# Samples' attention with the queries as weights in four column groups, a cache copy by batches, and a seventh chunk split ahead in the output projection

## The chip, the cores and the metric

The kernel runs on one core of one Trainium2 chip, in fp32 throughout. The metric is the device time of one execution in microseconds (us); three runs of the kernel before gave a median of 2682.03 us. TensorE (PE) multiplies, VectorE (DVE) and ScalarE (ACT) do elementwise work and empty the accumulators in PSUM, GpSimd (POOL) adds and issues DMAs, SyncE (SP) issues the loads of the weights.

## What is computed

Two decoder layers over 288 tokens: a prompt of 256 and 32 new sample tokens (8 batches of 4). Per layer:

```
n = RMSNorm(x)
q_s, k_s, v_s, q_r, k_r, v_r, g_r = split(n @ w_in)
o_swa = attention of q_s over k_s, v_s, window 128, 8 heads on 2 key/value heads, bias and sinks
o_ret = gated retention of q_r, k_r, v_r with a state per head (4 heads)
h = x + [o_swa || o_ret] @ w_o
x = h + SwiGLU(RMSNorm(h) @ w_gate_up) @ w_down
```

A sample token attends to 128 cached keys of its own batch (cache_k_win, cache_v_win) and to the new keys of its batch, with softmax over both and a sink. Outputs are y, the new windows of keys and values (for the samples: the cache shifted by 4 rows, then the 4 new rows) and the retention states.

## The kernel before

**The weight stream.** All products with weights have the weights at rest (128 x 128) and the 288 tokens moving. To keep fp32 accuracy, weights and activations are split in a high and a low part (`w_hi`, `w_lo`, `xg_hi`, `xg_lo`), and each block takes three matmuls (L982, L984, L986). The weights come in *rounds*: one round is 256 output columns over 2048 rows, in 8 *chunks* of 12 matmuls. SP loads, ACT writes `w_hi` (L363), DVE subtracts to get `w_lo` (L650), and PE multiplies. `w_hi` and `w_lo` are rings of four: chunk j can only be split once PE is through chunk j - 4. `split(r, j0, j1)` on ACT and on DVE splits chunks j0 to j1 of round r, and each engine's program is an order written by hand, in which the other work stands between the splits. `GLEAD` = 6 is the number of chunks of the next round that are split before that other work.

**The head groups.** After the first six rounds of w_in, a loop over four groups g runs four rounds (r to r + 3) per group. Between their chunks PE does the small matmuls of two attention heads, of the samples of two batches, and of one retention head. For the samples PE transposes the cached keys (`kcT`, L1096), ACT copies them out; PE multiplies with the keys at rest and 16 query columns moving (`sampT`, L1109), ACT copies that; PE transposes it back and adds the scores against the new keys (`samp_s`, L1117, L1119). DVE adds bias and mask and takes the maximum, ACT the exponential, DVE normalises. PE transposes the probabilities (`samp_pT`, L1134, L1135) and multiplies with the values at rest (`samp_pv`, L1142, L1147), which gives the output with the head's dimension on the partitions, as `cat_hi` and `cat_lo` want it. Small fp32 matmuls appear in the trace as two records each, transposes as one. All small results go through PSUM banks 4 to 7, whose users are listed in `BANK_USES`.

**The output projection.** Eight rounds r0 + R_O + 0 to 7 multiply `cat` by w_o. After each round DVE adds the accumulator to the residual (L909, semaphore `x_new`), ACT makes `xg_hi` (L375) and the squares (`pair_tmp`, L383), DVE makes `xg_lo` (L662), POOL adds the squares to `sq_acc` (L1306, L1308, semaphore `sq_added`, for which ACT's next squares wait). Then come the two gate/up rounds of FFN chunk 0 and a sum over partitions (L999).

**POOL's queue.** Per group it loads the bias, the cached keys and values and the states, and stores the new states. After the last group it copies the two cache windows from DRAM to DRAM in two DMAs of 992 KB (L1421), clears `sq_acc` (L1432) and enters the loop of additions.

Of the kernel before, what the change touches and what calls it, by code (L numbers as in the profile page):

```python
# [32 lines left out]
P = 128  # L33
# [3 lines left out]
DB = 8  # L37
# [33 lines left out]
for _name, _n in (("ident", P), ("ones", P), ("eps", 1), ("gammaC", RH), ("kdecay", RH * 2),  # L71
                  ("head_rows", 64), ("cos", T), ("sin", T), ("decay", RH * NP), ("qdecay", RH * NS), ("decay_s", RH * NS),
# [9 lines left out]
    "group": (("s0", 4), ("kcT", 5), ("s1", 4), ("sampT", 6), ("pT0", 5), ("samp_s", 6), ("pT1", 5),  # L82
              ("pv0", 6), ("pv1", 7), ("samp_pT", 5), ("samp_pv", 4), ("state_q", 6), ("o0", 6), ("o1", 7), ("kr_tok", 5),
# [26 lines left out]
def hybrid_trunk(nc, xT, cache_k, cache_v, state, rel_bias, w_in, sinks, sinksT, w_o, gainsT, w_gate_up,  # L110
# [4 lines left out]
    with ExitStack() as ctx:  # L115
        def sb(name, shape, dt=F32):
            return ctx.enter_context(nc.sbuf_tensor(name, shape, dt))
# [14 lines left out]
        sink_s = sb("sink_s", [64, DEPTH])  # L132
        bias_s = sb("bias_s", [64, P + NS])
# [29 lines left out]
        kc = over("kc", [P, 2, PAIR])  # L163
        vc = over("vc", [P, 2, PAIR])
        samp_sT = over("samp_sT", [P, 64])

        state_o = nc.alloc_sbuf_tensor_at("state_o", [P, PAIR], F32, offset=at[0])
        samp_p = over("samp_p", [64, P + NS])
        samp_pT = over("samp_pT", [P, 64])
        samp_pnT = over("samp_pnT", [NS, 64])  # L170
# [20 lines left out]
        kcT = over("kcT", [P, 4, P])  # L191
# [16 lines left out]
        def table(name, parts=P):  # L208
            a, b = TABLES[name]
            return cst[0:parts, a:b]  # L210

# [144 lines left out]
        def _(act):  # L356
# [60 lines left out]
            nc.scalar.activation(sink_s[:], ps[0:64, 5, 0:DEPTH], ACT.Copy).then_inc(bank_read[5], 1)  # L417
            act.drain().then_inc(rows_ready, 1)

            with act.Fori(0, DEPTH) as layer:  # L420
# [25 lines left out]
                with act.Fori(0, RH) as g:  # L446
# [14 lines left out]
                    filled(act, "kcT", layer, g)  # L461
                    copy_out(kcT[:], "kcT", 512)
# [12 lines left out]
                    def normalise(h):  # L475
# [11 lines left out]
                    filled(act, "sampT", layer, g)  # L487
                    copy_out(samp_sT[:], "sampT", 64)
# [6 lines left out]
                    nc.scalar.activation(samp_p[:], samp_p[:], ACT.Exp, bias=stats[0:64, 21:22],  # L495
                                         accum_out=stats[0:64, 22:23])
                    nc.scalar.activation(stats[0:64, 23:24], stats[0:64, 21:22], ACT.Exp,
# [17 lines left out]
                    copy_out(samp_pT[:], "samp_pT", 64, done=False)  # L515
                    copy_out(samp_pnT[:], "samp_pT", 64, NS, 64)
                    split(r + 2, 7, 8)
                    split(r + 3, 0, 1)
                    filled(act, "samp_pv", layer, g)
                    steady(act)  # L520
# [1002 lines left out]
```

## Time and profile before

| | |
|---|---|
| runs | 2682.03 us median (2680.91 to 2684.40, n = 3) |
| the profiled execution | 2685.05 us, its span 2683.5 us, mean granted clock 0.995 |
| PE busy | 2630.4 us, 98% |
| DVE, ACT, POOL busy | 56%, 47%, 7% |
| one group of the loop | 71.0 us, eight in all |
| output projection, first matmul to the sum for the FFN's norm | 127.6 us (layer 0), 124.7 us (layer 1) |

The page lists busy time by engine, the chain of work that ended last, and the groups of instructions with the idle time ahead of them. A matmul's own duration overlaps the next one's, so what a matmul costs in a stream is the distance from start to start: it is read from rows in order of time.

### The profile page before, as it was taken

The numbers are of one execution on the slowest core, as the hardware profiler recorded it, in microseconds if no ns is written. First come the engines' busy times: TensorE is split into PE (matmuls) and PEld (weight loads), VectorE is DVE, ScalarE is ACT, GpSimd is POOL, SyncE is SP. The second block draws the span as 40 slices with busy tenths as digits, with TensorE's granted clock in tenths as the row PEclk, the third lists the DMA queues.
The fourth block names the chain that finished last, engine by engine and source line by source line (L and its number), as shares of the span: only waits on it lengthen the run. The fifth ranks groups of instructions, "written<-read, shape, count | busy, mean of one in ns | idle before, by whom it ended". The sixth has DMA issues, their size and how long they took to land.

```text
span 2683.5 us, 53800 instructions
## 1 busy us (share of the span) xinstructions
PE 2630.4 (98%) x19722; PEld 2596.1 (97%) x19722; DVE 1491.9 (56%) x2387; ACT 1249.6 (47%) x2237; POOL 174.5 (7%) x222
## 2 busy tenths in 40 slices
PE   6999999999999999999999999999999999999997
PEld 6999999999999999999999999999999999999997
DVE  6566665555555555444455666555555555545445
ACT  4455554444444444444444555444444444444443
POOL 5300001000000000000020000110000000000000
PEclk9999999999999999999999999999999999999998
DMA  6655555555555555555555555554555555555554
GB/s 209 202 196 188 186 175 174 160 165 164 162 169 164 157 171 164 160 164 162 163 184 168 192 195 194 186 161 153 171 164 164 164 164 164 164 159 163 164 168 141
DMA packets 429939, 459.02 MB, mean 171 GB/s; under 512 B 19349, under 2 KB 418029, under 8 KB 429872
## 3 DMA queue, kind: packets, MB, share of 16 engines
q1 hardware_dynamic: 407488, 404.38, 49.2%
q0 software_dynamic: 18400, 48.42, 5.3%
q10 hardware_dynamic: 3984, 5.34, 0.6%
q8 instruction: 41, 0.67, 0.1%
q14 instruction: 26, 0.21, 0.0%
HBM read 436.12 MB, written 27.54 MB: 173 GB/s over the span
## 4 chain that ended last, share of the span: by engine, by line
PE 60%; issue 33%; DVE 3%; DVEq 1%; DMA 1%; POOLq 1%; ACT 1%; ACTq 0%; POOL 0%; SPq 0%
PE ps L982 19%; PE ps L984 18%; PE ps L986 18%; DVE w_lo L650 1%; DVE xg_lo L662 1%; DMA new_rs<-st 1%; PE ps L1223 1%; PE ps L1160 1%; PE ps L1232 1%; DVEq L910 1%; DMA raw<-w_in 0%; PE ps L1181 0%; ACT w_hi L363 0%; PE ps L1147 0%; POOLq L1309 0%
## 5 line engine op out<-in xcount | busy, mean ns | idle before, releaser
L650 DVE TENSOR_TENSOR w_lo<-raw,w_hi 128x512 fp32r<-128x512 f32 x1572 | 1067.3, 687 | 910.9 <-ACT w_hi L363 892.6
L363 ACT ACTIVATE w_hi<-raw 128x512 fp32r<-128x512 f32 x1572 | 960.9, 620 | 1105.3 <-PE ps L986 1085.8
L982 PE MATMUL ps<-xg_hi,w_hi 128*128 128x288 f32 x4224 | 1259.2, 298 | 18.7 <-DVE w_lo L650 14.5
L984 PE MATMUL ps<-xg_lo,w_hi 128*128 128x288 f32 x4224 | 1249.2, 296 | 0.0
L986 PE MATMUL ps<-xg_hi,w_lo 128*128 128x288 f32 x4224 | 1248.3, 296 | 0.0
L982 PEld LDWEIGHTS ps<-xg_hi,w_hi 128*128 128x128 f32 x4224 | 795.2, 188 | 25.7 <-DVE w_lo L650 12.6
L984 PEld LDWEIGHTS ps<-xg_lo,w_hi 128*128 128x128 f32 x4224 | 796.5, 189 | 0.5
L986 PEld LDWEIGHTS ps<-xg_hi,w_lo 128*128 128x128 f32 x4224 | 795.6, 188 | 0.0
L982 PE MATMUL ps<-cat_hi,w_hi 128*128 128x288 f32 x1024 | 305.5, 298 | 9.2 <-DVE w_lo L650 8.8
L984 PE MATMUL ps<-cat_lo,w_hi 128*128 128x288 f32 x1024 | 303.2, 296 | 0.0
L986 PE MATMUL ps<-cat_hi,w_lo 128*128 128x288 f32 x1024 | 303.0, 296 | 0.0
L982 PE MATMUL ps<-hid_hi,w_hi 128*128 128x288 f32 x896 | 265.7, 296 | 0.0
L984 PE MATMUL ps<-hid_lo,w_hi 128*128 128x288 f32 x896 | 264.3, 295 | 0.0
L986 PE MATMUL ps<-hid_hi,w_lo 128*128 128x288 f32 x896 | 264.1, 295 | 0.0
L982 PEld LDWEIGHTS ps<-cat_hi,w_hi 128*128 128x128 f32 x1024 | 192.9, 188 | 12.4 <-DVE w_lo L650 12.3
L984 PEld LDWEIGHTS ps<-cat_lo,w_hi 128*128 128x128 f32 x1024 | 193.2, 189 | 0.1
L986 PEld LDWEIGHTS ps<-cat_hi,w_lo 128*128 128x128 f32 x1024 | 192.9, 188 | 0.0
L982 PEld LDWEIGHTS ps<-hid_hi,w_hi 128*128 128x128 f32 x896 | 168.2, 188 | 0.0
L984 PEld LDWEIGHTS ps<-hid_lo,w_hi 128*128 128x128 f32 x896 | 168.2, 188 | 0.0
L986 PEld LDWEIGHTS ps<-hid_hi,w_lo 128*128 128x128 f32 x896 | 168.2, 188 | 0.0
L1306 POOL TENSOR_TENSOR sq_acc<-sq_acc,pair_tmp 128x288 f32<-128x288 f32 x32 | 26.3, 821 | 1804.5 <-ACT pair_tmp L383 1768.4
L662 DVE SCALAR_TENSOR_TENSOR xg_lo<-x_res,gains,xg_hi (+1 forms) x80 | 61.3, 809 | 58.0 <-ACT xg_hi L375 58.0
(201 smaller groups left out, 1241.8 us busy)
## 6 DMA issues: line engine op xcount, KB each, us to landing
raw<-w_gate_up SPq DMA_DIRECT2D x352, 512.0 KB, 3.6
raw<-w_in SPq DMA_DIRECT2D x178, 512.0 KB, 3.6
raw<-w_down SPq DMA_DIRECT2D x160, 512.0 KB, 3.7
raw<-w_o SPq DMA_DIRECT2D x64, 512.0 KB, 3.9
st<-state POOLq DMA_DIRECT2D x16, 1024.0 KB, 7.9
new_rs<-st POOLq DMA_DIRECT2D x16, 1024.0 KB, 5.9
raw<-w_down SPq DMA_DIRECT2D x32, 256.0 KB, 2.9
yT<-x_res ACTq DMA_DIRECT2D x4, 576.0 KB, 3.1
```

Of the source, the lines that this page charges most:

```text
L363: nc.scalar.activation(w_hi[q][:, 0:n, :], raw[s][:, n * (j % 2):n * (j % 2) + n, :], ACT.Copy).then_inc(hi_ready[q], 1)
L650: nc.vector.tensor_tensor(w_lo[q][:, 0:n, :], raw[s][:, n * (j % 2):n * (j % 2) + n, :], w_hi[q][:, 0:n, :].bitcast(F32), ALU.subtract).th ...
L662: ins = nc.vector.scalar_tensor_tensor(xg_lo[:, bass.ds(t + c, 1), :], x_res[:, bass.ds(t + c, 1), :], gains[:, norm, bass.ds(t + c, 1)], ...
L910: dve.drain().then_inc(x_new, 1)
L982: nc.tensor.matmul(out, w_hi[q][:, t, cols], x_hi[:, x, :], start=(k == 0), stop=False, skip_group_check=True)
L984: nc.tensor.matmul(out, w_hi[q][:, t, cols], x_lo[:, x, :], start=False, stop=False, skip_group_check=True)
L986: ins = nc.tensor.matmul(out, w_lo[q][:, t, cols], x_hi[:, x, :], start=False, stop=(k == kts - 1), skip_group_check=True)
L1160: ins = nc.tensor.matmul(bank("state_q", PAIR, NS, 0, NS * j), q_own[:, d, NS * b:NS * b + NS], st[:, 2 * b + d, :], start=(h + d == 0), s ...
L1223: ins = nc.tensor.matmul(bank("ret_st", PAIR, P, PAIR * d), kr_tok[:, b, P * d:P * d + P], vr_tok[:, b, :], start=(b == 0), stop=(b == 1))
L1232: ins = nc.tensor.matmul(bank(f"st{b}", PAIR, P, PAIR * d), k_own[:, b % OWN, P * d:P * d + P], v_stack[:], start=True, stop=True)
L1306: nc.gpsimd.tensor_tensor(sq_acc[:], sq_acc[:], pair_tmp[:, 0, :], ALU.add)
```

## The change

Three edits. (1) The samples' scores take the queries as weights, 32 columns in each of four column groups ("strips": key/value head and batch), with the cached keys, which now arrive transposed from the host's layout (`cache_kT`), moving; the transposes L1096 and the product `sampT` with their two copies on ACT go. The values' product takes the probabilities as weights in the same way, so its result has the rows on the partitions and is copied (`samp_o`) and transposed (`samp_oT`) back. Bias, sink and mask tables have 128 rows, and the bias of the new keys is added to the mask once, at the start. (2) The cache windows are copied batch by batch inside POOL's loop of additions, behind each pair of additions: 16 DMAs of 124 KB per layer. (3) In the output projection a seventh chunk is split ahead of the residual work, and ACT makes the squares before `xg_hi`.

```diff
-                    pe.wait_ge(group_loaded, done * 48 + 48)
-                    fill("kcT")
-                    for b in range(2):
-                        for kv in range(KV):
-                            ins = nc.tensor.transpose(bank("kcT", P, P, PAIR * b + P * kv),
-                                                      kc[:, b, P * kv:P * kv + P], ident)
...
-                    copied(pe, "kcT", layer, g)
-                    fill("sampT")
-                            ins = nc.tensor.matmul(bank("sampT", 16, P, c0), kcT[:, 2 * b + kv, :],
-                                                   samp_q[:, c0:c0 + 16], start=True, stop=True)
...
+                    pe.wait_ge(group_loaded, done * 48 + 48)
                     fill("samp_s")
-                    nc.tensor.transpose(bank("samp_s", P, 64), samp_sT[:], ident)
+                    for strip in range(4):
+                        kv, b = strip // 2, strip % 2
+                        nc.tensor.matmul(bank("samp_s", P, 32, 0, 32 * strip), samp_q[:, 32 * kv:32 * kv + 32],
+                                         kcT[:, 2 * b + kv, :], start=True, stop=True)
+                    for strip in range(4):
+                        ins = nc.tensor.matmul(bank("samp_s", NS, 32, P, 32 * strip), samp_q[:, 32 * kv:32 * kv + 32],
                                                kT[:, kv, NP:T], start=True, stop=True)
...
                     fill("samp_pv")
+                    for strip in range(4):
+                        nc.tensor.matmul(bank("samp_pv", P, 32, 0, 32 * strip), samp_pnT[:, 32 * strip:32 * strip + 32],
+                                         v_tok_s[:, P * (strip // 2):P * (strip // 2) + P], start=True, stop=False)
+                    for strip in range(4):
+                        ins = nc.tensor.matmul(bank("samp_pv", P, 32, 0, 32 * strip),
+                                               samp_pT[:, 32 * strip:32 * strip + 32], vc[:, b, P * kv:P * kv + P],
+                                               start=False, stop=True)
                     in_pair(r + 2, 0, pair + 1, 5, 6)
+                    copied(pe, "samp_pv", layer, g)
+                    is_filled(nc.tensor.transpose(bank("samp_oT", P), samp_o[:], ident), "samp_oT")
...
+                split(r0 + R_O, GLEAD, GLEAD + 1)
                 with act.Fori(0, 4) as i:
-                        split_on(r0 + R_O + i * 2 + c, GLEAD)
+                        split_on(r0 + R_O + i * 2 + c, GLEAD + 1)
                         act.wait_ge(x_new, n + 1)
-                        residual_pair(i * 4 + 2 * c, layer * 2 + 1, n + 8)
+                        pair_squares(i * 4 + 2 * c, n + 8)
+                        pair_hi(i * 4 + 2 * c, layer * 2 + 1)
...
                 with dve.Fori(0, 4) as i:
-                        split_on(r0 + R_O + i * 2 + c, GLEAD)
+                        split_on(r0 + R_O + i * 2 + c, GLEAD + 1, GLEAD)
                         add_to_residual(c, r0 + R_O + i * 2 + c, i, c)
+                        split(r0 + R_O + i * 2 + c + 1, GLEAD, GLEAD + 1)
                         lo_of_pair(i * 4 + 2 * c, layer * 2 + 1, layer * 16 + i * 2 + c + 8)
...
                     with pool.Fori(0, KT // 2) as i:
                         add_squares(layer * 16 + 8 * part + 8 + i)
+                        if part == 0:
+                            for w_new, w_old in ((new_ks, cache_k), (new_vs, cache_v)):
+                                pool.dma_start(w_new[bass.ds(layer, 1), bass.ds(i, 1), 0:WIN - DT].rearrange(
+                                    "l b w k d -> w (l b) (k d)"), w_old[bass.ds(layer, 1), bass.ds(i, 1), DT:WIN]
```

How the instructions stand in the programs (an x behind a row is its number; matmul shapes are output partitions x columns; ISA and register rows are waits and counters):

PE in a head group, the samples' pieces only, before (`kc` and `vc` are the cached keys and values, `cst` the identity):

```order
L1069 MATMUL ps<-kT,q_head 128x256
L1096 MATMUL ps<-cst,kc 128x128 x4
...
L1109 MATMUL ps<-samp_q,kcT 128x16 x4
...
L1076 MATMUL ps<-cst,probs_79 128x128 x3
L1117 MATMUL ps<-cst,samp_sT 64x128
L1119 MATMUL ps<-kT,samp_q 32x32 x2
...
L1142 MATMUL ps<-samp_pnT,v_tok_s 128x32
L1147 MATMUL ps<-samp_pT,vc 128x16 x2
...
L1160 MATMUL ps<-st,q_own 32x256 x16
```

and after, in the same stretch:

```order
L1074 MATMUL ps<-kT,q_head 128x256
...
L1081 MATMUL ps<-cst,probs_78 128x128 x3
L1107 MATMUL ps<-kcT,samp_q 32x128 x4
L1111 MATMUL ps<-kT,samp_q 32x32 x4
...
L1134 MATMUL ps<-v_tok_s,samp_pnT 32x128 x4
L1138 MATMUL ps<-vc,samp_pT 32x128 x4
...
L1146 MATMUL ps<-cst,samp_o 128x128
L1154 MATMUL ps<-st,q_own 32x256 x16
```

Two interruptions of the weight stream are gone, three remain at their places, and a transpose stands ahead of the states' product.

DVE in the output projection, one pass of the loop before, from the last chunk ahead of the residual:

```order
L650 TENSOR_TENSOR w_lo<-raw,w_hi 128x512 x2
L291 REGISTER_ALU
L909 ISA
L909 TENSOR_TENSOR x_res<-ps,x_res 128x576
L660 ISA
L662 ISA x2
L662 SCALAR_TENSOR_TENSOR xg_lo<-x_res,gains,xg_hi 128x288
L662 ISA x2
```

and after:

```order
L654 TENSOR_TENSOR w_lo<-raw,w_hi 128x512 x2
L296 REGISTER_ALU
L912 ISA
L912 TENSOR_TENSOR x_res<-ps,x_res 128x576
L654 TENSOR_TENSOR w_lo<-raw,w_hi 128x512
L664 ISA
L666 ISA x2
L666 SCALAR_TENSOR_TENSOR xg_lo<-x_res,gains,xg_hi 128x288
```

Chunk 6 of the next round has moved from behind the pair of `xg_lo` to ahead of it; chunk 7 still follows it.

POOL after the last group, before:

```order
L1421 DMA new_ks<-cache_k 124x8x256
L1421 DMA new_vs<-cache_v 124x8x256
L303 ISA
L1432 MEMSET sq_acc 128x288
L1434 UNCONDITIONAL_BRANCH
L1306 TENSOR_TENSOR sq_acc<-sq_acc,pair_tmp 128x288
L1308 TENSOR_TENSOR sq_acc<-sq_acc,pair_tmp 128x288
```

and after:

```order
L1427 MEMSET sq_acc 128x288
L1429 UNCONDITIONAL_BRANCH
L1300 TENSOR_TENSOR sq_acc<-sq_acc,pair_tmp 128x288
L1302 TENSOR_TENSOR sq_acc<-sq_acc,pair_tmp 128x288
L1433 DMA new_ks<-cache_k 16x1984
L1433 DMA new_vs<-cache_v 16x1984
```

The copies have moved behind the additions of each pass, and one is now 16 rows of 1984 numbers instead of 992 rows of 256.

## Rows read from the trace of the kernel before

**Rows 1.** Windows: busy us and (x records) per engine, clock, DMA share, GB/s.
```profile
600.00:1000.00 400.00, 400.00 (x3015) 400.00 (x3014) 217.27 (x314) 177.17 (x284) 0.00 (x0) 1.00 0.54 165
427.00:431.00 4.00, 3.40 (x15) 3.40 (x16) 2.96 (x4) 1.62 (x4) 1.07 (x1) 0.63 0.25 61
```
**Rows 2.** PE's waits over the whole span: total, times, longest.
```profile
PE ps L982 <- DVE w_lo L650: 23.3, 17, 6.1
```
**Rows 3.** PE in order of time, a group's scores: start us, duration us.
```profile
256.05 0.60 PE L1096 MATMUL ps<-cst,kc 128*128 128x128 f32 x4
256.41 0.38 PE L982 MATMUL ps<-xg_hi,w_hi 128*128 128x288 f32 x1
...
262.24 0.96 PE L1109 MATMUL ps<-samp_q,kcT 128*128 128x16 f32 x8
263.04 0.38 PE L982 MATMUL ps<-xg_hi,w_hi 128*128 128x288 f32 x1
...
268.23 0.27 PE L1117 MATMUL ps<-cst,samp_sT 128*64 128x128 f32 x1
268.44 0.26 PE L1119 MATMUL ps<-kT,samp_q 128*32 128x32 f32 x4
268.62 0.40 PE L982 MATMUL ps<-xg_hi,w_hi 128*128 128x288 f32 x1
```
**Rows 4.** PE, the same group: the samples' values, and the states' product in strips.
```profile
285.27 0.40 PE L1142 MATMUL ps<-samp_pnT,v_tok_s 32*128 32x32 f32 x2
...
286.96 0.38 PE L982 MATMUL ps<-xg_hi,w_hi 128*128 128x288 f32 x1
...
288.73 1.93 PE L1160 MATMUL ps<-st,q_own 128*32 128x256 f32 x32
```
**Rows 5.** Weight loads (PEld) and DVE just after the scores, same group.
```profile
258.95 0.19 PEld L982 LDWEIGHTS ps<-xg_hi,w_hi 128*128 128x128 f32 x1 [0.46 <-DVE w_lo L650]
...
258.21 1.29 DVE L650 TENSOR_TENSOR w_lo<-raw,w_hi 128x512 fp32r<-128x512 f32 x2
...
264.54 0.68 DVE L650 TENSOR_TENSOR w_lo<-raw,w_hi 128x512 fp32r<-128x512 f32 x1
```
**Rows 6.** PE in the output projections of layers 0 and 1: ends and stops.
```profile
387.67 0.51 PE L982 MATMUL ps<-cat_hi,w_hi 128*128 128x288 f32 x1
...
427.60 0.40 PE L982 MATMUL ps<-cat_hi,w_hi 128*128 128x288 f32 x1 [3.23 <-DVE w_lo L650]
...
442.45 0.40 PE L982 MATMUL ps<-cat_hi,w_hi 128*128 128x288 f32 x1 [0.27 <-DVE w_lo L650]
...
515.26 0.65 PE L999 MATMUL ps<-sq_acc,cst 128*128 128x288 f32 x2
...
1711.92 0.51 PE L982 MATMUL ps<-cat_hi,w_hi 128*128 128x288 f32 x1
...
1836.61 0.65 PE L999 MATMUL ps<-sq_acc,cst 128*128 128x288 f32 x2
```
**Rows 7.** POOL in order of time, output projection of layer 0.
```profile
423.51 0.80 POOL L1306 TENSOR_TENSOR sq_acc<-sq_acc,pair_tmp 128x288 f32<-128x288 f32 x1 [17.86 <-issue]
...
439.98 0.89 POOL L1306 TENSOR_TENSOR sq_acc<-sq_acc,pair_tmp 128x288 f32<-128x288 f32 x1 [11.77 <-ACT pair_tmp L383]
```
**Rows 8.** ACT in order of time, the same stretch.
```profile
419.49 1.15 ACT L363 ACTIVATE w_hi<-raw 128x512 fp32r<-128x512 f32 x2 [5.12 <-DMA raw<-w_o]
...
425.45 0.68 ACT L383 ACTIVATE pair_tmp<-x_res 128x576 f32 x1 [1.94 <-POOLq L1309]
...
438.36 0.96 ACT L375 ACTIVATE xg_hi<-x_res,gains  x2 [1.84 <-DVEq L910]
```
**Rows 9.** DVE in order of time, one round of the same stretch.
```profile
437.16 0.75 DVE L909 TENSOR_TENSOR x_res<-ps,x_res 128x576 f32 x1
439.68 1.51 DVE L662 SCALAR_TENSOR_TENSOR xg_lo<-x_res,gains,xg_hi  x2 [1.77 <-ACT xg_hi L375]
441.11 1.29 DVE L650 TENSOR_TENSOR w_lo<-raw,w_hi 128x512 fp32r<-128x512 f32 x1
```

More of the change, by code:

```diff
@@ L81 @@
     "pre": (("rms_mix", 4), ("k_tok", 7), ("v_tok", 5), ("v_tok_s", 7)),
-    "group": (("s0", 4), ("kcT", 5), ("s1", 4), ("sampT", 6), ("pT0", 5), ("samp_s", 6), ("pT1", 5),
-              ("pv0", 6), ("pv1", 7), ("samp_pT", 5), ("samp_pv", 4), ("state_q", 6), ("o0", 6), ("o1", 7), ("kr_tok", 5),
+    "group": (("s0", 4), ("s1", 4), ("pT0", 5), ("samp_s", 6), ("pT1", 5),
+              ("pv0", 6), ("pv1", 7), ("samp_pT", 5), ("samp_pv", 4), ("samp_oT", 7), ("state_q", 6), ("o0", 6), ("o1", 7), ("kr_tok", 5),
               ("kr_copies", 4), ("ret_s", 5), ("vr_tok", 4), ("vr_copies", 5), ("ret_st", 4),
@@ L107, in use_number, with hybrid_trunk @@
     return at
-def hybrid_trunk(nc, xT, cache_k, cache_v, state, rel_bias, w_in, sinks, sinksT, w_o, gainsT, w_gate_up,
+def hybrid_trunk(nc, xT, cache_kT, cache_k, cache_v, state, rel_bias, w_in, sinks, sinksT, w_o, gainsT, w_gate_up,
                  w_down, tables, onehot, yT, new_kp, new_vp, new_rp, new_ks, new_vs, new_rs):
@@ L210, in table, with samp_heads @@
             return cst[0:parts, a:b]
+        def samp_heads(kv):
+            rows = bank("samp_oT", 64, P, 64 * kv).rearrange("p (x n) -> p x n", n=16)
+            return rows[:, 0:4:3, :].rearrange("p b (h t) -> p b h t", h=4)
         ident, ones, eps, cos, sin = (table(n) for n in ("ident", "ones", "eps", "cos", "sin"))
@@ L519, in _ @@
                     filled(act, "samp_pv", layer, g)
+                    copy_out(samp_o[:], "samp_pv", P)
+                    filled(act, "samp_oT", layer, g)
                     steady(act)
@@ L1248, in _ @@
                     sum_partitions("gnorm", layer, [rot_tmp[:, v, :] for v in range(2)], g)
-                copied(pe, "samp_pv", layer, RH - 1)
+                copied(pe, "samp_oT", layer, RH - 1)
                 pe.wait_ge(cat_ready, layer * RH + RH - 1)
@@ L1503 @@
     ins = {
-        "xT": x.T, "cache_k": cache_k_win, "cache_v": cache_v_win, "state": state_ret, "rel_bias": rel_bias,
+        "xT": x.T, "cache_kT": np.asarray(cache_k_win).reshape(DEPTH, RH, 2, WIN, KV, P).transpose(0, 1, 5, 2, 4, 3),
+        "cache_k": cache_k_win, "cache_v": cache_v_win, "state": state_ret, "rel_bias": rel_bias,
         "w_in": w_in, "sinks": sinks, "sinksT": np.asarray(sinks).T, "w_o": w_o,
```

146 lines of the change are left out of this document (66 added, 80 removed).

## The prediction

> **What bounds the kernel now.** I read the busy shares first, then PE's waits, then PE in order of time inside one head group and inside the output projection, and last what DVE, ACT and POOL did at the places where PE stopped. In a window of the gate/up rounds PE is busy all of 400 us, DVE 217 and ACT 177 [rows 1]. So only what shortens PE's stream, or a stop in it, can pay. The stream has a steady price: where nothing interrupts it, 3015 matmuls take 400 us, 0.1327 us each, so a chunk of 12 takes 1.59 us and a round of 96 takes 12.74 us. Nearly all the waits that PE shows are for `w_lo`, 23.3 us in 17 times [rows 2], some of them at the start of the kernel and the rest mostly in the output projections.
>
> The output projections lose more than those waits, because PE also refills after a stop. From the first matmul to the sum for the FFN's norm there are 768 + 96 + 24 = 888 weight matmuls; at 0.1327 us that is 117.8 us. Layer 0 takes 515.26 - 387.67 = 127.6 us and layer 1 takes 1836.61 - 1711.92 = 124.7 us [rows 6]: 9.8 and 6.9 us too long, 16.7 us together.
>
> **The samples' attention, on PE.** All prices are distances from start to start, per group, and there are eight groups.
>
> Removed: the transposes of the cached keys, 256.41 - 256.05 = 0.36 us; the product `sampT`, 263.04 - 262.24 = 0.80 us; the transpose back and the scores against new keys, 268.62 - 268.23 = 0.39 us [rows 3]; the values' product, 286.96 - 285.27 = 1.69 us [rows 4].
>
> Added: the products in strips. The trace has such products already: L1160 writes four column groups, and 32 records of 256 columns take 1.93 us, 0.060 us each [rows 4]. A record of 128 columns would be half of that, 0.030 us, if the columns set the pace; L1119, in two column groups with 32 columns, takes 0.18 us for four records with the change of tile form behind them [rows 3], about 0.045 each, so a floor by issue cannot be much lower than 0.03. I take 0.033 us per record of 128 columns and 0.025 for 32. Each product is two records. The scores are 8 records of 128 and 8 of 32: 0.26 + 0.20 us. A change of tile form costs about 0.1 us: L1117 is one transpose, and a transpose is 0.09 us (four in 0.36), but L1119, the first in another form, follows it after 0.21 us [rows 3]. With one change in and one out the scores take 0.66 us where 0.39 stood: +0.27. The values are 16 records of 128 columns, 0.53 us, with a change between the two halves (32 rows, then 128) and one behind: 0.73 us where 1.69 stood: -0.96. The transpose `samp_oT` adds 0.11. The transposes of the probabilities have 128 columns instead of 64, but leave one change of form out: 0. `sampT` goes whole: -0.80.
>
> The transposes of the keys I count at nothing. Behind the second scores PE already waits for chunk 7 of round r, 0.46 us on the weight loads, and the two splits that DVE makes there (0.65 us each) start only at 258.21, behind the softmax's maxima [rows 5]. That work starts when the first scores are done, which stand ahead of the transposes; with these gone PE comes 0.36 us earlier to the same wait. If DVE were early after all, 8 x 0.36 = 2.9 us more would be saved. Where `sampT` goes the splits are nearly late too: chunk 3 of that round, the tightest, is split by 264.54 + 0.68 = 265.22 [rows 5], and PE, which would go on at 262.24 instead of 263.04, would want it two chunks later, at 265.42.
>
> Per group: -0.80 + 0.27 - 0.96 + 0.11 = -1.38 us, in eight groups -11.0 us. The bounds: if strips did not overlap, a record would cost what one of L1109 does, 0.80 / 8 = 0.10 us [rows 3]; 24 records of 128 columns would cost 24 x 0.067 = 1.6 us more and the 8 small ones up to 0.16, so the group would be slower by 0.4 us, +3 us in all. At the other end every record at 0.025 and the keys' transposes saved: -1.38 - 0.2 - 0.36, some -15.5 us. The first half of the values' product uses a tile of 32 rows and 32 columns that no row shows; I give it L1160's price, the nearest.
>
> On ACT two copies go and one, `samp_o`, comes; PE has a whole chunk, 1.59 us, between the product and the transpose, which covers it. DVE has one small operation less. ACT's copy of the samples into `cat_hi` comes one chunk later, and DVE, queued behind it, reaches the next round's first split later by as much; PE wants that chunk only after the states' product and two chunks. The keys' load is as large as before.
>
> **The output projection.** Two kinds of stop cost PE time there, and a third may come, which I take in turn.
>
> First, the copies of the windows. In layer 0 ACT waits 5.12 us for a load of w_o, and in the next round 1.94 us for POOL [rows 8], whose first addition came 17.86 us late [rows 7], while two copies of 992 KB ran. PE stood 3.23 us [rows 6], and after that stop its clock was at the lower level, 1.2 GHz, for a while: 15 records in the 4 us around it at a mean clock of 0.63 [rows 1], where 3.4 us of full speed would hold 26, so some 1.4 us more. In the changed kernel the additions come first and each pass issues 124 KB twice, an eighth, with a round of 12.7 us before POOL is wanted again. These stops and the clock's loss should go: about 6 us in layer 0 and over 3 in layer 1.
>
> Second, a short stop in every round. PE stood 0.27 us for chunk 6 and started it at 442.45 [rows 6], so it wanted it by about 442.1. DVE split it at 441.11, behind `xg_lo`, and took 1.29 us [rows 9], where two such splits take 1.29 us elsewhere [rows 5]: POOL's additions, 439.98 and after [rows 7], ran beside it. With the seventh chunk ahead, DVE splits chunk 6 right behind the residual (437.16 + 0.75), by about 438.8, three microseconds early.
>
> What is late next is chunk 7. On the clock of this round: ACT gets `x_new` about 438.4, squares for 0.68 and makes `xg_hi` for 0.96 us, until 440.0 [rows 8]; DVE `xg_lo` 440.1 to 441.6 if it is slowed as it was (1.51 us), chunk 7 by 442.9 if that split is slowed too (1.29 us) [rows 9]. PE wants it a chunk after 442.1, at 443.7. So it is in time by 0.8 us, and by more if POOL, which starts its additions as early as 439.1, is done.
>
> The row on the split beside POOL (1.29 us instead of 0.65) agrees with a rule of the Trainium skill, SBUF — State Buffer, "Who interferes with whom": an operation of VectorE with two SBUF inputs and one of GpSimd that reads SBUF share a read port, and the one that comes second is blocked for the whole of the first. It speaks against squares ahead of `xg_hi`, for both additions now meet `xg_lo`. By the rule DVE would lose at most both additions, and chunk 7 would come about 443.0; by the rows 442.9. Either is in time.
>
> Of the 16.7 us I leave 0.4, the refill behind the sum at the two starts, and 0.3 for leftovers: -16.0 us. The lower bound is the long stops alone, -9 us.
>
> **The sum.** -11.0 - 16.0 = -27.0 us. The profiled execution took 2685.05 us, so it would take 2658; the median of the runs shown was 3.0 us lower, 2682.03, so the median would be 2655.0. The setup on POOL has half as many small DMAs, and the wait of PE for them at the start is for others: 0.
>
> **The rivals.** (a) The strips do not overlap, in the new tile forms or in all. Against it is L1160. The group then gives +3 instead of -11: 2669 us. (b) The splits do not keep up in the groups: like the keys' transposes, `sampT`'s 0.80 us only moves PE forward into a wait for `w_lo`. For it is the margin of 0.2 us; against it that all splits but one were on time. 8 x 0.8 = 6.4 us lost: 2661 us. (c) Chunk 7 takes chunk 6's place as the late one: the margin of 0.8 us is from rows with one state of POOL, and POOL now also writes the copies' descriptors there. The short stops stay, some 0.5 us in 14 rounds, 7 us: 2662 us. (d) Slower: a pass of POOL's loop with copies in it lasts as long as the pass behind the copies did, 17.86 us and two additions, about 19.6 us [rows 7]. ACT's squares, which now stand ahead of `xg_hi` and of chunk 7, wait for the addition before them, so each of seven rounds per layer would last 19.6 instead of 12.7 us: 14 x 6.9 = 97 us more, 2752 us. It decides as soon as a pass exceeds 12.7 us, that is when POOL is held over 11 us behind two DMAs. Against it: the copies are an eighth as large and in 16 rows instead of 992.
>
> **Chances.** Forecast 0.69, (a) 0.08, (b) 0.09, (c) 0.08, (d) 0.03, and 0.03 for several of them at once, so that nothing can be told. This kernel's times can be told apart from about 0.2%, 5.4 us. The forecast and (a) to (c) are all under 2676.6, faster by more than that. Faster 0.94, same 0.03, slower 0.03. The range goes from 2647 (the far bounds, -15.5 and -16.7, give 2650, and the runs of before scatter by some 3 us) to 2670, case (a).
>
> **What would show it.** Right: the records of L1107 and L1138 start about 0.03 us apart; no L982 of the w_o rounds carries a wait over 0.2 us; the stretch from the first w_o matmul to the norm's sum takes about 118 us in both layers at full clock; PEld still waits behind the second scores, by 0.8 instead of 0.46 us; a group takes about 69.6 us instead of 71.0. Wrong: strips 0.1 us apart (a); new waits for `w_lo` in rounds r + 1 (b) or a stop of 0.2 to 0.5 us in each w_o round at chunk 7 (c); a long idle of POOL ahead of its additions (d).

## The result, and the profile after

The changed kernel took 2647.57 us (median, 2645.96 to 2649.07, n = 4), the kernel before 2683.22 us (2680.91 to 2684.85, n = 4): ratio 0.9863, 95% interval 0.985 to 0.9876. That is 36 us faster, where 27 were forecast. In two more comparisons its ratio was 0.9871 (0.9855 to 0.9888) and 0.9864 (0.9849 to 0.9879). The profiled execution took 2649.07 us, its span 2647.5 us, at a clock of 0.995, the same as before.

Where the 36.0 us between the two spans lie, by the starts of the stages on PE (the rows add up to 35.6; of the rest, 0.3 us lies in the norm and the first matmuls of layer 1, which take 18.90 us before and 18.62 after):

| stretch | before, us | after, us | difference | forecast |
|---|---|---|---|---|
| one head group, eight in all | 71.03 | 69.20 | -1.83 x 8 = -14.6 | -11.0 |
| output projections, layers 0 and 1 | 127.59, 124.69 | 117.69, 117.69 | -9.9, -7.0 | -16.0 together |
| gate/up, each layer | 546.5 | 546.5 | 0 | 0 |
| down projections, layers 0 and 1 | 285.5, 286.0 | 283.3, 284.8 | -2.2, -1.2 | 0 |
| first weight matmul | 15.68 | 14.94 | -0.7 | 0 |

PE in order of time in the changed kernel (start us, duration us). First the pieces of one group: second scores of the heads, scores of the samples, transposes of their probabilities, values, transpose back; then the ends of the two output projections:

```profile
254.53 0.40 PE L987 MATMUL ps<-xg_hi,w_hi 128*128 128x288 f32 x1 [0.20 <-DVE w_lo L654]
...
263.03 0.42 PE L1107 MATMUL ps<-kcT,samp_q 128*32 128x128 f32 x8
263.27 0.24 PE L1111 MATMUL ps<-kT,samp_q 128*32 128x32 f32 x8
263.44 0.40 PE L987 MATMUL ps<-xg_hi,w_hi 128*128 128x288 f32 x1
...
276.36 0.27 PE L1126 MATMUL ps<-cst,samp_p 128*128 128x128 f32 x1
276.46 0.27 PE L1127 MATMUL ps<-cst,samp_p 128*32 128x128 f32 x1
276.49 0.38 PE L987 MATMUL ps<-xg_hi,w_hi 128*128 128x288 f32 x1
...
279.85 0.42 PE L1134 MATMUL ps<-v_tok_s,samp_pnT 32*32 32x128 f32 x8
280.20 0.43 PE L1138 MATMUL ps<-vc,samp_pT 128*32 128x128 f32 x8
280.56 0.40 PE L987 MATMUL ps<-xg_hi,w_hi 128*128 128x288 f32 x1
...
379.60 0.51 PE L987 MATMUL ps<-cat_hi,w_hi 128*128 128x288 f32 x1
...
497.29 0.40 PE L1004 MATMUL ps<-sq_acc,cst 128*128 128x288 f32 x1
...
1684.12 0.51 PE L987 MATMUL ps<-cat_hi,w_hi 128*128 128x288 f32 x1
...
1801.81 0.40 PE L1004 MATMUL ps<-sq_acc,cst 128*128 128x288 f32 x1
```

They answer to [rows 3, 4, 6]. The strips overlap: eight records of 128 columns take 263.27 - 263.03 = 0.24 us, 0.030 each in the mean, and eight of 32 columns 0.17 us, the change of form behind them included. The mean hides how: the first four records, one per column group, start nearly together, and the other four 0.13 us behind them. In a window that ends at 263.15 us only four have started:

```profile
263.03 0.32 PE L1107 MATMUL ps<-kcT,samp_q 128*32 128x128 f32 x4
```

The values take 280.56 - 279.85 = 0.71 us instead of 1.69. Both output projections take 117.69 us, and no L987 in them waits. Over the whole span PE waits for `w_lo` (total, times, longest) 14.9 us where it waited 23.3 [rows 2]:

```profile
PE ps L987 <- DVE w_lo L654: 14.9, 13, 5.8
```

The transposes of the probabilities were forecast at no change. The same piece in the kernel before, PE in order of time:

```profile
281.64 0.27 PE L1134 MATMUL ps<-cst,samp_p 64*128 64x64 f32 x1
281.75 0.22 PE L1135 MATMUL ps<-cst,samp_p 64*32 64x64 f32 x1
281.89 0.40 PE L982 MATMUL ps<-xg_hi,w_hi 128*128 128x288 f32 x1
```

There 0.25 us pass from the first transpose to the next weight matmul, now 0.13; with the way in, the piece is 0.20 us shorter.

The down projections contain no edit, and they became faster. Windows of the kernel before, two of 200 us, one in each layer's down projection (as in [rows 1], the number behind x is that of PE's records; one or two that an edge cuts count too):

```profile
1100.00:1300.00 200.00, 200.00 (x1503) 200.00 (x1501) 99.04 (x153) 88.38 (x152) 9.24 (x12) 1.00 0.54 163
2400.00:2600.00 200.00, 200.00 (x1502) 200.00 (x1501) 98.83 (x155) 89.41 (x155) 9.70 (x12) 1.00 0.54 163
```

and of the changed kernel, with the gate/up window of [rows 1] ahead:

```profile
600.00:1000.00 400.00, 400.00 (x3015) 400.00 (x3014) 217.31 (x314) 176.51 (x283) 0.00 (x0) 1.00 0.54 164
1100.00:1300.00 200.00, 200.00 (x1514) 200.00 (x1514) 100.13 (x156) 90.00 (x157) 9.70 (x12) 1.00 0.55 166
2400.00:2600.00 200.00, 200.00 (x1508) 200.00 (x1507) 99.52 (x156) 89.41 (x156) 9.68 (x12) 1.00 0.54 164
```

Gate/up has the same 3015 records. In the down projections 1514 and 1508 fit where 1503 and 1502 did, with PE busy all the time and at full clock in both. Measured from start to start over unbroken stretches, a weight matmul with `cat` or `hid` moving took 133.3 ns before, and after 132.2 ns in both output projections and the down projection of layer 0, but 132.8 in that of layer 1; with `xg` moving it took 132.8 in both kernels.

### The profile page after: what moved, and what is told of

Read it like the earlier page. It is cut to its first block, busy times and chain, and to the rows that moved or that the text cites. A ratio compares the mean times of both kernels' runs of the same rounds, so it can differ in the third digit from the quotient of the medians.

```text
span 2647.5 us, 53927 instructions
## 1 busy us (share of the span) xinstructions
PE 2603.3 (98%) x19754; PEld 2570.5 (97%) x19754; DVE 1485.6 (56%) x2387; ACT 1249.3 (47%) x2229; POOL 173.0 (7%) x235
## 4 chain that ended last, share of the span: by engine, by line
PE 66%; issue 31%; DVE 2%; POOLq 1%; DMA 0%; DVEq 0%; ACT 0%; SPq 0%; POOL 0%; ACTq 0%
PE ps L987 20%; PE ps L989 20%; PE ps L991 20%; PE ps L1217 1%; PE ps L1226 1%; PE ps L1154 1%; DVE xg_lo L666 0%; PE ps L1175 0%; DMA raw<-w_in 0%; DVE w_lo L654 0%; PE ps L1004 0%; PE ps L1205 0%; POOLq L1301 0%; POOLq L1303 0%; DVE x_res L965 0%
## 5 line engine op out<-in xcount | busy, mean ns | idle before, releaser
L987 PE MATMUL ps<-xg_hi,w_hi 128*128 128x288 f32 x4224 | 1261.7, 299 | 19.0 <-DVE w_lo L654 14.9
L987 PEld LDWEIGHTS ps<-xg_hi,w_hi 128*128 128x128 f32 x4224 | 795.4, 188 | 28.9 <-DVE w_lo L654 15.7
L987 PE MATMUL ps<-cat_hi,w_hi 128*128 128x288 f32 x1024 | 301.3, 294 | 0.0
L987 PE MATMUL ps<-hid_hi,w_hi 128*128 128x288 f32 x896 | 263.8, 294 | 0.0
L987 PEld LDWEIGHTS ps<-cat_hi,w_hi 128*128 128x128 f32 x1024 | 192.5, 188 | 0.1
L987 PEld LDWEIGHTS ps<-hid_hi,w_hi 128*128 128x128 f32 x896 | 168.3, 188 | 0.0
```

The costliest lines, as they stand in the source:

```text
L987: nc.tensor.matmul(out, w_hi[q][:, t, cols], x_hi[:, x, :], start=(k == 0), stop=False, skip_group_check=True)
```

## The experiments

The theory after the first comparison had three parts: the groups gain more than forecast on PE itself; the stops go as forecast, the long ones by edit 2 and the short ones by edit 3; and the pace of `cat` and `hid` follows their place in SBUF, which the change moved without meaning to (`cst`, `sink_s` and `bias_s`, which lie ahead of them, have new sizes). `cat_hi` began at byte 127136 of each partition, 32 behind a multiple of 128, and begins now at 127296, 64 behind one; `xg_hi` is at a multiple of 128 in both.

**One edit at a time.** The edits are shown shortened; lines in parentheses stand for more of the kernel. e1 is edit 1 alone:

```diff
 # the changed kernel
-                split(r0 + R_O, GLEAD, GLEAD + 1)
-                        pair_squares(i * 4 + 2 * c, n + 8)
-                        pair_hi(i * 4 + 2 * c, layer * 2 + 1)
+                        residual_pair(i * 4 + 2 * c, layer * 2 + 1, n + 8)
-                        if part == 0:
-                            (a copy of one batch)
+                (the two copies of 992 KB ahead of the loop)
```

> The kernel before with edit 1 alone (the samples' attention in strips, with its new tables), window copies and chunk 6 as before. Theory: a group of the loop takes 69.2 us instead of 71.0 (8 x -1.83 = -14.7), the weight matmuls with cat or hid moving go from 133.3 to 132.2-132.8 ns apart because the tables' new sizes move these tiles in SBUF (-1.7 in the output projections, -3.4 in the down projections), the start -0.7: about -20.5 us together, and the long and short stops of the output projections stay as they were. Rival, by the forecast's own terms: the groups alone, -11 us, and matmuls at 133.3 ns where they stood.

2665.20 us against 2684.59, ratio 0.9936 (0.9921 to 0.9951): 19.4 us of the 20.5 expected, where the rival had 11. The group takes 69.21 us (scores at 112.34 and 181.55). `cat` and `hid` run at 132.2 ns, at 132.8 in layer 1's down projection and in a part of each output projection. The output projections take 125.3 and 127.9 us, with the long and the short stops in them. So the groups' gain and the change of pace both come with edit 1.

e2 is edit 2 alone, e3 edit 3 alone, each in the kernel before:

```diff
 # e2
-                    pool.dma_start(w_new[layer, all batches], w_old[...])
+                        if part == 0: (in the loop of additions)
+                            pool.dma_start(w_new[layer, batch i], w_old[...])
 # e3
+                split(r0 + R_O, GLEAD, GLEAD + 1)
+                        pair_squares(i * 4 + 2 * c, n + 8)
+                        pair_hi(i * 4 + 2 * c, layer * 2 + 1)
-                        residual_pair(i * 4 + 2 * c, layer * 2 + 1, n + 8)
```

> The kernel before with edit 2 alone: the cache windows copied batch by batch behind POOL's additions. Theory (the forecast's first kind of stop): the long stops go, ACT waits for no load of w_o over 1 us, the stop of 0.27 us in each round stays, so the output projections take about 122 us each instead of 127.6 and 124.7 and the kernel is 8 to 9 us faster. Rival d' (POOL held by the descriptors in the loop): stops of a microsecond or more in each round, not faster.

> The kernel before with edit 3 alone: the seventh chunk split ahead, squares before xg_hi, the two big copies where they were. Theory (the forecast's second kind of stop): the 14 short stops of 0.5 us go, -7 us, the long ones stay. Rival: with squares first, xg_hi and chunk 7 stand behind ACT's wait for POOL's first addition, which the copies hold for 17.9 us, so the long stop grows by the 5 to 10 us that ACT now passes without chunk 7: between -2 us and slower by 10.

e2: 2669.76 us against 2683.81, ratio 0.995 (0.9934 to 0.9967), 14.1 us faster, five more than expected. e3: 2678.79 us, ratio 0.9982 (0.9973 to 0.9992), 5.0 us faster. PE in e2, first matmul, only stop and sum of the output projection of layer 0:

```profile
387.17 0.51 PE L982 MATMUL ps<-cat_hi,w_hi 128*128 128x288 f32 x1
...
410.22 0.40 PE L982 MATMUL ps<-cat_hi,w_hi 128*128 128x288 f32 x1 [0.28 <-DVE w_lo L650]
...
506.26 0.40 PE L999 MATMUL ps<-sq_acc,cst 128*128 128x288 f32 x1
```

119.09 us, and 119.06 in layer 1: one short stop in each layer, not seven. e2 does not touch the splits, so the short stops come and go with the place of the copies. POOL and DVE show how. The kernel before in a later round, POOL's second addition and DVE's split of chunk 6:

```profile
467.54 0.84 POOL L1308 TENSOR_TENSOR sq_acc<-sq_acc,pair_tmp 128x288 f32<-128x288 f32 x1
...
467.64 1.29 DVE L650 TENSOR_TENSOR w_lo<-raw,w_hi 128x512 fp32r<-128x512 f32 x1
```

and e2 in the same place:

```profile
447.70 0.68 DVE L650 TENSOR_TENSOR w_lo<-raw,w_hi 128x512 fp32r<-128x512 f32 x1
...
447.79 1.25 POOL L1308 TENSOR_TENSOR sq_acc<-sq_acc,pair_tmp 128x288 f32<-128x288 f32 x1 [0.33 <-issue]
```

Before, the addition starts 0.10 us ahead of the split, takes 0.84, and the split 1.29 us. In e2 it starts 0.09 us behind, and it is the addition that is stretched, to 1.25 us, while the split takes 0.68. The other rounds agree: before, the addition is ahead in each of the six rounds per layer that have a short stop; in e2 it is ahead in the first round of each layer alone, the one with the stop, and behind in the seven others. This is the rule of the Trainium skill that the prediction named (SBUF — State Buffer, "Who interferes with whom"): the one that comes second is blocked. What the prediction missed is that two tenths of a microsecond decide who is second. In the loop that also issues DMAs POOL starts its second addition 0.33 us after the end of the first instead of 0.14 (0.15 in the first pass, which no copy of the loop precedes); why the issue is longer there the trace does not say.

e3 kept the long stops, as it kept the copies: POOL's first addition and ACT's wait for w_o in layer 0 are those of [rows 7, 8]. POOL in e3:

```profile
422.12 0.80 POOL L1310 TENSOR_TENSOR sq_acc<-sq_acc,pair_tmp 128x288 f32<-128x288 f32 x1 [17.53 <-issue]
```

PE stopped 1.54 and 2.75 us in layer 0 and 2.90 in layer 1, where it stopped 0.86 and 3.23, and 2.98 before, so the rival's growth by 5 to 10 us did not come. The short stops were gone. Its projections take 124.9 and 123.1 us, 4.3 less together, where 7 were expected; the interval of the times, 2.1 to 7.2 us, holds both. Some 1.5 us of what is missing is the clock behind the long stop of layer 1. Windows of 4 us from the end of the stop, of e3:

```profile
1747.00:1751.00 4.00, 3.97 (x19) 3.97 (x20) 1.78 (x3) 0.63 (x1) 0.00 (x0) 0.61 0.55 171
```

and of the kernel before:

```profile
1750.50:1754.50 4.00, 4.00 (x30) 4.00 (x31) 3.04 (x4) 1.69 (x4) 0.59 (x1) 1.00 0.33 110
```

In e3 a part of the window runs at the lower level, 1.2 GHz (mean 0.61), and holds 11 matmuls less; before, the clock stays at full behind a stop as long. Why it fell in the one and not in the other these rows do not show.

e11 is the changed kernel without edit 3, e7 the changed kernel with `xg_hi` ahead of the squares:

```diff
 # e11
-                split(r0 + R_O, GLEAD, GLEAD + 1)
-                        pair_squares(i * 4 + 2 * c, n + 8)
-                        pair_hi(i * 4 + 2 * c, layer * 2 + 1)
+                        residual_pair(i * 4 + 2 * c, layer * 2 + 1, n + 8)
 # e7
-                        pair_squares(i * 4 + 2 * c, n + 8)
                         pair_hi(i * 4 + 2 * c, layer * 2 + 1)
+                        pair_squares(i * 4 + 2 * c, n + 8)
```

> The changed kernel without edit 3: six chunks ahead, xg_hi before the squares, edits 1 and 2 kept. Forecast's terms: the 14 short stops of 0.5 us come back, 7 us slower than the changed kernel. Theory from edit 2 alone (the short stops go with the big copies, since POOL's second addition then comes behind DVE's split and not ahead of it): one stop per layer, the output projections about 118.2 us each instead of 117.7, about 1 us slower.

> The changed kernel with xg_hi ahead of the squares again, the seventh chunk still ahead. Theory: with edit 2 POOL's additions are never late, and chunk 7 has slack in either order, so nothing changes, within 1 us, and the output projections stay at 117.7 us each. Rival (the order of squares carries part of the gain): short stops for chunk 7 come back, 0.2 to 0.5 us in 14 rounds, 3 to 7 us slower.

e11: 2651.43 us, ratio 0.9882 (0.9865 to 0.9898), against 0.9871 (0.9855 to 0.9888) for the changed kernel on the same chip. The times do not tell them apart; the trace does: its projections take 118.51 and 118.28 us, 0.8 and 0.6 more than 117.69, with one stop in each. Of this 0.2 us is pace, since the last rounds of layer 0 ran at 132.8 ns. So on top of edit 2, edit 3 is worth 1.2 us and not 7. e7: 2646.92 us, ratio 0.9866 (0.9849 to 0.9882), projections 117.69 and 117.69: the order of the squares is worth nothing.

**What in the copies made the long stops.** e8 issues the copies ahead of the loop, as before, but cut as edit 2 cuts them:

```diff
-                    pool.dma_start(w_new[layer, all batches], w_old[...])
+                for b in range(DB):
+                        pool.dma_start(w_new[layer, b] as 16 rows of 1984, w_old[...])
```

> The kernel before, with the window copies still issued all at once ahead of the additions, but as 16 copies of 16 rows of 1984 numbers, as edit 2 cuts them. Theory A (the number of descriptors, 992 rows per copy, holds POOL 17.86 us and loads the queues): POOL is held under 8 us, ACT's wait for w_o of 5.12 us shrinks to under 2, the output projection of layer 0 takes about 122 us. Theory B (the two megabytes at once take the DMA engines from the loads of w_o): POOL is free early, but ACT's wait for w_o stays at 4 us or more and the projection takes 125 us or more.

One run: 2675.57 us. POOL is free earlier (first issue 398.48, first addition 416.38, idle 7.43 us ahead of it instead of 17.86), and ACT waits for no load of w_o at all. The largest stop of PE in layer 0:

```profile
422.83 0.40 PE L982 MATMUL ps<-cat_hi,w_hi 128*128 128x288 f32 x1 [0.62 <-DVE w_lo L650]
```

The projections take 122.3 and 122.0 us; what is left is the seven short stops per layer (some 0.5 us each with the refill). Theory A fits and theory B is refuted: the same two megabytes, issued within 10 us, no longer delay the weights when they come as 16 rows per copy. Their issue now takes 10 us instead of the 4.2 of before, which e8 does not separate from the number of rows. Spreading them over the loop, as edit 2 does, then brings the projections from 122 to 119.1 us, by moving POOL's second additions, which ended the short stops.

**The key transposes.** e6 puts four unused transposes where they stood:

```diff
                     scores(0)
+                    free(pe, "pT0", layer, g)
+                    for b in range(4):
+                        nc.tensor.transpose(bank("pT0", P, P, P * (b % 2)), kT[:, b // 2, 0:P], ident)
```

> The changed kernel with four transposes of 128 columns at the place behind the first scores where the key transposes stood; their results go to a free bank and are not used. Forecast (they were hidden by the wait behind the second scores): the group stays at 69.2 us. Rival: they cost their 0.36 us, the group takes 69.55 us and the kernel is 2.9 us slower.

One run: 2647.94 us, group 69.20 us (250.88 to 320.08 for the first scores). Hidden, as forecast. PEld's waits in the changed kernel behind the first and the second scores:

```profile
251.82 0.19 PEld L987 LDWEIGHTS ps<-xg_hi,w_hi 128*128 128x128 f32 x1 [0.43 <-DVE w_lo L654]
...
254.53 0.19 PEld L987 LDWEIGHTS ps<-xg_hi,w_hi 128*128 128x128 f32 x1 [0.60 <-DVE w_lo L654]
```

and in e6, where only the second is left:

```profile
254.44 0.19 PEld L987 LDWEIGHTS ps<-xg_hi,w_hi 128*128 128x128 f32 x1 [0.46 <-DVE w_lo L654]
```

From the first scores to the matmul behind the second it is 3.55 us in the one and 3.56 in the other. The transposes' 0.36 us became a wait [rows 5], though not at the second scores alone, where the prediction looked for it: there the wait grew from 0.46 to 0.60 us, not to 0.8, and the first scores have one of 0.43.

**The pace.** Only unused bytes were added, so that tiles move and no instruction differs:

```diff
 # e4: before; e5, e10: after, with 8 and 16 words
+        sb("pad", [P, 40])
         rstd = sb("rstd", [P, T])
 # e9, e13: after, 16 + 16 and 8 + 24 words; e12: e4 with 16 + 16
+        sb("pad_a", [P, 16])
         xg_hi = sb("xg_hi", [P, KT, T], F32R)
         xg_lo = sb("xg_lo", [P, KT, T], F32R)
+        sb("pad_b", [P, 16])
```

> The kernel before with one unused tile of 160 bytes per partition ahead of rstd, so that cat_hi, cat_lo, hid_hi and hid_lo lie where the changed kernel has them (0 instead of 32 bytes behind a multiple of 64), and not one instruction different. Theory (the address sets the pace): weight matmuls with cat or hid moving 132.2 to 132.8 ns apart instead of 133.3, in the down projections -3.4 us and in the output projections -1.7, together about -5 us. Rival (the pace comes from the other work that runs beside it): nothing changes, 133.3 ns, within 1 us.

> The changed kernel with one unused tile of 32 bytes per partition ahead of rstd, so that cat and hid lie 32 bytes behind a multiple of 64 again, as in the kernel before. Theory (address): their matmuls are 133.3 ns apart again and the kernel is about 5 us slower than the changed one. Rival (the other work beside it): as the changed kernel, within 1 us.

> The changed kernel with cat and hid 64 bytes further on, at a multiple of 128, as xg is. Theory (the place within 128 bytes sets the pace: 132.8 at 0, 133.3 at 32, 132.2 at 64, 132.5 at 96): their matmuls are 132.8 ns apart in both projections of both layers, about 2 us slower than the changed kernel. Rival (only a place 32 bytes behind a multiple of 64 is slow): 132.2 to 132.8 as in the changed kernel, within 1 us.

> The changed kernel with xg_hi and xg_lo moved by 64 bytes, from a multiple of 128 to 64 behind one, everything else at its place. Theory A (a moving operand 64 bytes behind a multiple of 128 is the fastest, as cat and hid in the changed kernel): gate/up goes from 132.8 to 132.2 ns per matmul, and with the rounds of w_in about -4.6 to -6 us against the changed kernel. Theory B (only 32 bytes behind a multiple of 64 is slow): no change, within 1 us.

> The changed kernel with xg 32 bytes behind a multiple of 128, where cat and hid were slow in the kernel before. Theory: gate/up at 133.3 ns instead of 132.8 (+4.5 us, and about +1 in w_in), so about 2654 us. Rival (32 is slow for cat and hid for another reason, for example that they are 32 bytes behind while xg, the other tile of the same stretch of program, is at 0): 132.8 ns as before, 2648 us.

> The kernel before with xg, cat and hid all 64 bytes behind a multiple of 128, and not one instruction different. Theory (place within 128 bytes): gate/up goes from 132.8 to 132.2 ns (8160 matmuls, -4.6 us), the projections from 133.3 to 132.2 (7300 matmuls, -8 us), w_in a little: 12 to 13 us faster than before. Rival (the pace of gate/up goes with the changed program): at most the 3.5 us that moving cat and hid alone gave.

> The changed kernel once more, unaltered, to see whether the pace of one stage is the same in another execution. In the execution shown the down projection of layer 0 ran at 132.2 ns per matmul and that of layer 1 at 132.8. Theory (a stage takes one of two paces anew in each execution): at least one stage shows the other pace this time, and the times scatter by 2 to 3 us. Rival (the pace belongs to the place in the program): the same paces as before.

> The changed kernel, for comparison on one chip with the run that follows: about 2648 us; the output projections at 132.2 ns per matmul, the down projections at 132.2 or 132.8, anew in each execution.

> The changed kernel with xg 64 bytes behind a multiple of 128, as in e9: 2641.5 us, 6 to 7 us under the changed kernel on this chip, with 132.2 ns in all stages. Rival (e9's gain was the chip's): within 2 us of the changed kernel.

The places are bytes behind a multiple of 128; the pace is ns per weight matmul, start to start, in one profiled execution each; "down" gives layers 0 and 1.

| kernel | xg at | cat, hid at | gate/up | w_o | down | median us (ratio to before on the same chip, interval) |
|---|---|---|---|---|---|---|
| before | 0 | 32 | 132.8 | 133.3 | 133.3, 133.3 | |
| e4 | 0 | 64 | 132.8 | 132.2 | 132.8, 132.2 | 2681.13 (0.999, 0.9981 to 0.9999) |
| e12 | 64 | 64 | 132.2 | 132.2 | 132.2, 132.2 | 2676.94 (0.9975, 0.9966 to 0.9984) |
| after | 0 | 64 | 132.8 | 132.2 | 132.2, 132.8 | 2647.57 (0.9863, 0.985 to 0.9876) |
| after_again | 0 | 64 | 132.8 | 132.2 | 132.8, 132.8 | 2649.14 (0.9871, 0.9855 to 0.9888) |
| after_third | 0 | 64 | 132.8 | 132.2 | 132.2, 132.8 | 2647.53 (0.9864, 0.9849 to 0.9879) |
| e5 | 0 | 96 | 132.8 | 132.5 | 132.5, 132.5 | 2648.58 (0.9871, 0.9856 to 0.9886) |
| e10 | 0 | 0 | 132.8 | 132.8 | 132.8, 132.8 | 2649.76 (0.9875, 0.9859 to 0.9892) |
| e13 | 32 | 64 | 133.3 | 132.8 | 132.8, 132.8 | 2655.90 (one run) |
| e9 | 64 | 64 | 132.2 | 132.2 | 132.2, 132.2 | 2641.30 (0.9844, 0.9831 to 0.9857) |
| e9_again | 64 | 64 | 132.2 | 132.2 | 132.2, 132.2 | 2641.36 (0.9843, 0.983 to 0.9857) |

The windows show it without any other step. The kernel before with all tiles at 64 (e12), gate/up, then the two down projections:

```profile
600.00:1000.00 400.00, 400.00 (x3028) 400.00 (x3027) 218.40 (x316) 178.36 (x285) 0.00 (x0) 1.00 0.54 165
1100.00:1300.00 200.00, 200.00 (x1515) 200.00 (x1514) 97.67 (x153) 88.46 (x153) 8.08 (x10) 1.00 0.53 164
2400.00:2600.00 200.00, 200.00 (x1514) 200.00 (x1514) 100.10 (x156) 90.04 (x157) 9.68 (x12) 1.00 0.55 168
```

The changed kernel with `xg` at 32 (e13), gate/up and a down projection:

```profile
600.00:1000.00 400.00, 400.00 (x3002) 400.00 (x3001) 216.57 (x314) 176.52 (x282) 0.00 (x0) 1.00 0.53 163
1100.00:1300.00 200.00, 200.00 (x1508) 200.00 (x1507) 99.69 (x156) 89.81 (x156) 9.72 (x12) 1.00 0.53 163
```

The changed kernel with `cat` and `hid` at 0 (e10), the two down projections:

```profile
1100.00:1300.00 200.00, 200.00 (x1509) 200.00 (x1508) 99.68 (x156) 89.81 (x156) 9.69 (x12) 1.00 0.54 165
2400.00:2600.00 200.00, 200.00 (x1509) 200.00 (x1508) 99.07 (x155) 89.98 (x156) 9.69 (x12) 1.00 0.54 164
```

and the kernel before with `cat` and `hid` at 64 (e4):

```profile
1100.00:1300.00 200.00, 200.00 (x1509) 200.00 (x1508) 97.46 (x152) 87.48 (x151) 8.07 (x10) 1.00 0.52 163
2400.00:2600.00 200.00, 200.00 (x1514) 200.00 (x1514) 100.30 (x157) 90.00 (x156) 9.70 (x12) 1.00 0.53 165
```

So the place of the moving operand sets the pace: 132.8 ns at 0, 133.3 at 32, 132.5 at 96, and at 64 132.2 where all tiles lie there. It does so for `xg` as for `cat`, and in the kernel before as in the changed one. Theory B of e9, that only 32 is slow, is refuted by e9 and e10, and the rivals of e4, e12 and e13 by the paces there. But the expectation of e5 as it stood (133.3 ns wherever a tile lies 32 behind a multiple of 64) is refuted too: at 96 the pace is 132.5, and the time is that of the changed kernel within what these runs can tell. e10 had the paces that were expected; its time is 0.6 us above that of the changed kernel on the same chip (2649.14), where 2 were expected, and that is too little to tell. Other places than these four were not tried.

One thing stays open. With `cat` and `hid` at 64 and `xg` at 0, a down projection ran at 132.2 ns in 8 and at 132.8 in 8 of the 16 layers of the eight profiles with these places (e1, e4, e6, e7, e11 and the changed kernel three times), anew in each execution, and in e1 and e11 output projections changed from one pace to the other on their way. With `xg` at 64 all were at 132.2 (e9 twice, e12), with `xg` at 32 all at 132.8 (e13). So the place alone does not decide at 64. That the stream before it takes part would fit these runs, but the pace also changed within a stream, in e11 with no stop near it; what decides, no run shows.

e4 gained 3.5 us of the expected 5, e12 7.2 of 12 to 13. The paces came as expected in both, and a part was lost in the output projections (253.7 and 252.9 us for both layers, 252.3 before, where the pace alone should have saved 1.7): in layer 1 PE stopped up to 4.82 us in e4 and 4.27 in e12, 2.98 before, and the mean clock of the 4 us behind these stops was 0.50 and 0.57, against 1.00. For e12 this explains 2.3 us in its profiled execution, which at 2673.40 us was the fastest of eleven; what held the slower ones (up to 2680.50) no trace shows.

e9, with `xg` at 64, beats both kernels: 2641.36 us against 2647.53 for the changed kernel on one chip (2641.18 to 2642.70 and 2646.71 to 2648.34), 6.2 us less from 128 unused bytes per partition.

## Why the prediction was too small

The mechanisms were right where the prediction named them, and the signs came: strips at 0.030 us per record of 128 columns, no wait in the rounds of w_o, projections of 117.7 us in both layers, PEld waiting behind the second scores (0.60 us, where 0.8 was forecast). No rival took place: not (a), not (b), not (c); and for (d), POOL issues a copy in 0.52 us and its additions wait for ACT alone. But the gain was 36.0 us and not 27.0. Of the 9.0 us too many, 3.6 are the groups, 3.4 the down projections, 0.9 the output projections and 1.0 the starts of the two layers. The steps that failed:

**The sum per group, -1.83 instead of -1.38 us, 3.6 us in all.** Term by term, forecast and measured: `sampT` -0.80, -0.88 (the refill behind it went too); scores +0.27, +0.12 (records at 0.030 and 0.021 us, not 0.033 and 0.025, the change of form behind them included); values -0.96, -0.97; `samp_oT` +0.11, +0.10; key transposes 0, 0; transposes of the probabilities 0, -0.20. The largest error is that last one: the prediction saw that a change of form goes, and set it off against the columns, though its own price for a change was 0.1 us at each end. That the change of form is what was saved is read from the forms in the rows (64x64 before, 128x128 after); no run separates it. The next is the scores, by 0.15 us. The prediction reasoned that "a floor by issue cannot be much lower than 0.03" us per record, from four records of 32 columns with the change behind them; the eight of L1111 all start within 0.05 us, and most of their 0.17 us comes behind the last start.

**"The stream has a steady price: where nothing interrupts it, 0.1327 us each."** The row behind it is a window of gate/up alone [rows 1]. The same view of the down projections, which was not read, gives 133.3 ns. The prediction could not have known from before's rows which way the pace would go, but it took the stages without an edit to be fixed, while edit 1 changed the sizes of tables that lie ahead of `cat` and `hid`. The pace is worth 3.4 us in the down projections, and in the output projections 1536 x 1.1 ns = 1.7 us.

**The output projections, -16.9 us.** The size was right, the working was not, so that the total came out close to -16.0 is in part luck. It is 15.2 us of stops and 1.7 of pace, and the stops were divided wrongly. The prediction held the short stops to be a matter of chunk 6's place in DVE's order, worth 7 us, which only edit 3 removes. Edit 2 alone removes 14.1 us (e2), edit 3 alone 4.3 (e3), and edit 3 behind edit 2 only 1.2 (e11). The failed step is the reading of the 1.29 us split: POOL's additions were taken as a load that lies there in any case, where it was the order of two starts 0.1 us apart. One more reading was loose: the 17.86 us ahead of POOL's first addition are its idle time, not its delay. ACT had written the squares for it by 407.50 + 0.67 = 408.17, so it came 15.3 us late; only the price of rival (d) hangs on that.

**The start, -0.7 us**, is no effect of the change: the first weight matmul came at 15.68 us in the profile of before, and between 14.3 and 15.2 in all the other profiles, those of the kernel before with moved tiles (e4, e12) among them.

## What to carry to other kernels

Read the price of the dense stream in every stage, not in one: where two stages of equal matmuls differ by half a per cent, try the place of their moving operand before anything else, and count every tile whose address an edit moves as touched by it. An edit that is priced for one stop can remove another by the way, as edit 2 did with the short ones by shifting a start by two tenths of a microsecond, so each edit should be tried alone. Look at how a copy within DRAM is cut, and not only at its bytes: here the same bytes in 16 rows per copy instead of 992 left the loads beside them alone (one run).

## What the runs showed of the hardware

- A 128x128 by 288-column fp32r matmul ran at 132.2, 132.5, 132.8 or 133.3 ns by the byte at which the moving operand's rows (1152 bytes each) begin; worked out in cycles of the full clock, 2.4 GHz, three such matmuls take 952, 954, 956 or 960. Places 0, 32, 64 and 96 behind a multiple of 128 were tried.
- With `cat` and `hid` at 64 and `xg` at 0, a whole stage ran at either of two paces, 132.2 or 132.8 ns, anew in each execution; what decides is open.
- Products in four column groups, of fp32: four records, one per group, start nearly together, the next four 0.13 us later at 128 columns; eight take 0.24 us, and eight of 32 columns 0.17 us with the change of form behind them.
- A DVE split and a POOL addition that start 0.1 us apart: the second is stretched, the split from 0.68 to 1.29 us or the addition from 0.84 to 1.25.
- 16 copies of 124 KB in 16 rows each, issued within 10 us, let the loads of w_o through without a wait of ACT (e8, one run); two of 992 KB in 992 rows each, issued within 4.2 us, made ACT wait 5.12 us.
